# A 46-column unit with its high and low weights in one stationary tile, and a last projection whose last two weight rows go tile by tile

## The chip, the cores and the metric

The kernel runs on one core of one Trainium2 chip, as one program. The metric is the device time of a run in microseconds (us); of several runs the median counts. A separate execution is recorded by the hardware profiler: every instruction of each engine with start and length. The engines are TensorE (PE, with weight loads as PEld), VectorE (DVE), ScalarE (ACT), GpSimd (POOL) and SyncE (SP), which here issues the DMAs.

## What is computed

Two blocks of a language model on a sequence of 512 tokens of width 1024 in float32. The first (a short convolution, a gated delta rule and a convolutional feed-forward) is not touched by the change. The second is:

```python
def second_block(x, w_in, norm_g, pool_w, pool_scale, fox_bf, w_out, final_g):
    ...
        h = rmsnorm_2(x, norm_g[layer])
        z = jnp.einsum('bld,dc->blc', h, w_in[layer])
        (pv, pg, dq, dk, dv, dg, iq, ik, iw, fq, fk, fv, fg, ff) = split_columns(z)
        a_out = pool_mixer(pv, pool_w[layer], pool_scale[layer]) * jax.nn.silu(pg)
        b_o = dsa_mixer(..., iq.reshape(B, L, IDX_HEADS, IDX_DIM), ik, iw * idx_w_scale, topk)
        ...
        log_f = jax.nn.log_sigmoid(ff.astype(jnp.float32) + fox_bf[layer].astype(jnp.float32))
        c_o = fox_mixer(fq..., fk..., fv..., log_f)     # F = cumsum(log_f); logit + F[t] - F[s]
        ...
        mixed = jnp.concatenate([a_out, b_out, c_out], axis=-1)
        x = x + jnp.einsum('blc,cd->bld', mixed, w_out[layer])
    return rmsnorm_2(x, final_g)
```

`dsa_mixer` scores each key for each query, `score = sum_h iw[h] * relu(iq[h] . ik)` over 8 index heads of 32, takes the 128 best keys and attends to those. `ik` has 32 columns of the projection, `iw` 8, and `ff`, the forget gates of `fox_mixer`, 6: these 46 columns are the thin unit.

## The kernel before

**Weights in two parts.** Each float32 weight matrix is used as a rounded high part and the rest, the low part, and so are the activations. A product is then three matmuls of 128x512: high by high, low by high, high by low. SyncE loads a unit of weights (128 columns by 1024 rows, as 128 partitions x 8 x 128) into one of four buffers of `raw`; ScalarE copies it to `whi` (L1190, `split`); VectorE, for some units GpSimd, subtracts to get `wlo` (L1653, L2534). `whi` and `wlo` have two buffers each, so the split of a unit waits for the end of the unit two before it (`unit_done`), and the unit itself waits for its low part (`split_ready`). TensorE multiplies in `unit` (L679), 24 matmuls with the eight blocks of activations, into one of four banks of `gb`.

**The projection into the second block** has the units of `Z_UNITS`, u = 0, 1, 2 and so on: unit 0 is the thin one, units 1 and 2 are `iq`, then come the keys, queries, values and gates of the heads. A unit is written in four quarters, and `schedule()` puts small jobs behind quarters: `put(u, m, job)` stands behind quarter m (from 0) of unit u. Each engine goes through the same plan and does its own share of each job (`beside`), at its own place among its splits and its reads of finished units (`z_out`, in the loop at quarter 1 of the next unit). All waits are semaphores, and every engine does its instructions in the order in which they are written. What reads a finished unit scales it by the norm of each token; this row comes from sums of squares (`third_sums`, four float32 matmuls with `ones`, after quarter 1 of unit 0), VectorE's `sum_positions`, GpSimd's power and the job `spread 2`.

The jobs of the thin unit:
- `turn_iw` (2, 1): ScalarE copies the 32 rows of `ik` four times into `ik4` (`dec`, L1562), TensorE transposes the unit (L1032), and VectorE takes `iw` and `ff` from it (L2199 to L2205). `spread 3` (2, 2) makes the row of the final norm.
- `log_f` (3, 1): the logarithm of the forget gates, a long chain of small VectorE operations (L1658 to L2217).
- `cum_f` (4, 1): TensorE sums them over the positions (L1038, L1039) into bank 3 of `gd`, and VectorE copies the 24 columns out (L2224, semaphore `f_tok`), ahead of its `z_out` in that place.
- `turn_f` (4, 3): TensorE transposes the sums (L1044), ScalarE copies them to `frow` (L1569, `f_rows`), and SyncE sends them to DRAM and back as rows.
- `four`: four score products at once (L1061), one for each of four index heads, one in each bank of `gd`, from slot 14 = (3, 2) on; ScalarE applies relu (L1576), and VectorE adds them up weighted (`score`, L2232, L2235). The third group, n = 8 at (4, 2), uses bank 3 and waits for `f_tok`; the fourth, n = 12 at (5, 0), waits for `f_rows`.

**The last projection** (from L1137) has eight rows of `w_out` as moving operands and the four tiles of 128 tokens as stationary ones; all four tiles of 128x1024 results stand in the eight banks at once. `products(i, c)` is the work of weight row i on tile c, six matmuls (L1158). Weight rows go in the order of i, and within one all four tiles. After a tile's last matmul (`tile_done`) ScalarE squares it and sums (L1637), GpSimd makes the factor (L2546, L2547), VectorE multiplies by factor and `final_g` (L2386), and SyncE sends the 512 KB (L658).

## Time and profile before

| what | us |
|---|---|
| runs of the kernel before | 1306.73, 1307.70, 1307.81 |
| median | 1307.7 |
| span of the profiled execution | 1305.9 |
| TensorE busy in it | 1288.1 (99%) |
| VectorE busy | 822.2 (63%) |
| ScalarE busy | 560.4 (43%) |
| GpSimd busy | 240.9 (18%) |

For the profiled execution the profile gives its span, from the first to the last instruction or transfer, and no separate time; what a run takes around its span is in the runs and not in the span. Matmuls overlap, so the length of one is more than the distance to the next, and a busy TensorE need not be at its peak. The second block's projection begins at 1001.3 us of the span, the last projection near 1255.

### The profile page before, as it was taken

Reading aid. Unit: us, or ns where it says so; the run is one execution under the profiler, and the core shown is the slowest. Engines: PE = TensorE matmul, PEld = TensorE weight load, DVE = VectorE, ACT = ScalarE, POOL = GpSimd, SP = SyncE. Lnnn points to the kernel's source line nnn. Section 1 sums busy time; section 2 is a strip of 40 time slices with the busy share of each in tenths; the row PEclk is TensorE's granted clock in tenths of the full one; section 3 lists DMA queues with packets and bytes.
Section 4 is the critical chain, followed back from the end, with each engine's and each line's share of the span. In section 5 each row is a group of like instructions: output and inputs, shape, how many; then the busy total and the mean of one; then the engine's idle time right before and its main releaser. Section 6 shows DMA issues by size and latency. Waiting matters only on the chain.

```text
span 1305.9 us, 20263 instructions
## 1 busy us (share of the span) xinstructions
PE 1288.1 (99%) x6833; PEld 1029.2 (79%) x6833; DVE 822.2 (63%) x1694; ACT 560.4 (43%) x1010; POOL 240.9 (18%) x491
## 2 busy tenths in 40 slices
PE   8999999999999999999999999999999999999998
PEld 6877878878788788888788888888887766767786
DVE  6976667676676753445477773377755688885823
ACT  5654535445454432223344442244444454434422
POOL 2513304032140400001300000000022234433210
PEclk9999999999999999999999999999999999999999
DMA  6323232232232223333233323433234332222221
GB/s 184 90 66 90 80 86 76 79 87 71 83 88 65 79 81 97 96 96 97 81 104 99 97 74 97 122 93 97 72 91 112 90 107 86 66 65 65 65 65 65
DMA packets 210052, 114.44 MB, mean 88 GB/s; under 512 B 7696, under 2 KB 206671, under 8 KB 210005
## 3 DMA queue, kind: packets, MB, share of 16 engines
q1 hardware_dynamic: 210005, 113.84, 30.2%
q8 instruction: 26, 0.43, 0.1%
q14 instruction: 21, 0.17, 0.0%
HBM read 111.70 MB, written 2.13 MB: 87 GB/s over the span
## 4 chain that ended last, share of the span: by engine, by line
PE 91%; DVE 6%; issue 1%; ACT 1%; DMA 0%; POOL 0%; SPq 0%; POOLq 0%; DVEq 0%; ACTq 0%
PE gb L679 77%; PE gb L1158 2%; PE gd L1158 1%; PE gd L1109 1%; PE gd L1086 1%; PE gd L1099 1%; DVE wlo L1653 1%; DVE selb L2246 1%; PE gd L787 1%; PE gd L870 1%; PE gd L879 1%; DVE small L2245 0%; PE gd L775 0%; DVE selb L2235 0%; PE gd L858 0%
## 5 line engine op out<-in xcount | busy, mean ns | idle before, releaser
L679 PE MATMUL gb<-act_a,whi 128*128 128x512 f32 x2656 | 898.6, 400 | 1.2 <-POOL wlo L2534 0.7
L679 PEld LDWEIGHTS gb<-act_a,whi 128*128 128x128 f32 x2656 | 499.6, 188 | 118.6 <-issue 16.7
L679 PE MATMUL gb<-act_a,wlo 128*128 128x512 f32 x1416 | 552.7, 390 | 0.0
L1653 DVE TENSOR_TENSOR wlo<-raw,whi 128x1024 fp32r<-128x1024 f32 (+1 forms) x198 | 239.2, 1208 | 161.0 <-ACT whi L1190 158.2
L1190 ACT ACTIVATE whi<-raw 128x1024 fp32r<-128x1024 f32 (+1 forms) x211 | 217.2, 1029 | 234.1 <-PE gb L679 203.2
L679 PEld LDWEIGHTS gb<-act_a,wlo 128*128 128x128 f32 x1416 | 266.9, 189 | 48.5 <-issue 1.0
L679 PE MATMUL gb<-act_b,whi 128*128 128x512 f32 x432 | 152.4, 393 | 0.1
L679 PEld LDWEIGHTS gb<-act_b,whi 128*128 128x128 f32 x432 | 81.1, 188 | 17.4 <-DVE qc L1930 0.5
L2488 POOL TENSOR_TENSOR zs<-zs,ca 128x512 f32<-128x512 f32 x3 | 4.2, 1400 | 321.7 <-ACT ca L1193 321.7
L679 PE MATMUL gb<-act_b,wlo 128*128 128x512 f32 x128 | 49.9, 390 | 0.0
L2439 POOL TENSOR_TENSOR elt<-Ti,Ue 128x60 f32<-128x60 f32 (+14 forms) x120 | 44.3, 370 | 27.8 <-DVE Ti L1775 13.5
L2442 POOL TENSOR_TENSOR Ue<-Ue,elt 128x60 f32<-128x60 f32 (+14 forms) x120 | 39.1, 326 | 9.4
L1604 ACT ACTIVATE pT<-gd 128x512 f32<-128x512 f32 (+3 forms) x24 | 10.5, 438 | 61.0 <-PE gd L1099 40.2
L2534 POOL TENSOR_TENSOR wlo<-raw,whi 128x1024 fp32r<-128x1024 f32 x13 | 31.1, 2393 | 22.0 <-ACT whi L1190 22.0
L1289 ACT ACTIVATE ob<-gd,hc 128x128 f32<-128x128 f32 x24 | 8.8, 368 | 55.7 <-DVE Rr L1880 55.7
L2126 DVE TENSOR_TENSOR Yb<-gb,Vt 128x512 f32<-128x512 f32 x22 | 15.2, 691 | 24.9 <-PE gb L679 24.9
L2471 POOL TENSOR_TENSOR zs<-zs,ca 128x512 f32<-128x512 f32 x3 | 5.6, 1858 | 134.8 <-ACT ca L1193 134.8
L2456 POOL TENSOR_TENSOR rr<-ss,rr 128x4 f32<-128x4 f32 x8 | 1.6, 201 | 150.7 <-DVE ss L1899 150.7
L679 PEld LDWEIGHTS gb<-act_b,wlo 128*128 128x128 f32 x128 | 24.0, 188 | 4.6
L2165 DVE TENSOR_TENSOR xT<-xT,gb 128x512 f32 (+1 forms) x16 | 11.0, 688 | 26.3 <-PE gb L679 26.3
L2245 DVE MAX8 small<-selb 128x8 f32<-128x256 f32 (+2 forms) x48 | 26.6, 555 | 0.6
L2450 POOL TENSOR_TENSOR rr<-ss,eps_one 128x4 f32<-128x4 f32 x8 | 1.6, 202 | 134.1 <-DVE ss L1823 134.1
(508 smaller groups left out, 1573.2 us busy)
## 6 DMA issues: line engine op xcount, KB each, us to landing
raw<-in_w_in_dram SPq DMA_DIRECT2D x102, 512.0 KB, 3.4
raw<-in_w_up_dram SPq DMA_DIRECT2D x44, 512.0 KB, 3.6
raw<-in_w_down_dram SPq DMA_DIRECT2D x16, 384.0 KB, 3.1
raw<-in_w_down_dram SPq DMA_DIRECT2D x16, 320.0 KB, 3.0
raw<-in_w_a_out_dram SPq DMA_DIRECT2D x8, 512.0 KB, 3.4
raw<-in_w_b_out_dram SPq DMA_DIRECT2D x8, 512.0 KB, 3.4
raw<-in_w_o_dram SPq DMA_DIRECT2D x8, 512.0 KB, 3.4
raw<-in_w_out_dram SPq DMA_DIRECT2D x8, 512.0 KB, 3.5
```

The costliest lines, as they stand in the source:

```text
L679: ins = pe.matmul(gb[:, b, :], l, r, start=(first and m == 0), stop=(last and m == len(todo) - 1))
L787: ins = pe.matmul(gd[:, 3, c * P:c * P + P], KT[:, c, :], QT[:, c, :], start=True, stop=True)
L870: pe.matmul(gd[:, 3, 0:P], Ui[:, c, :], rhs, start=True, stop=True).then_inc(vn_done, 1)
L879: pe.matmul(gd[:, 1, 0:P], AT[:, c, :], vn[:], start=True, stop=True).then_inc(av_done, 1)
L1158: ins = pe.matmul(place(c, half), l, r, start=False, stop=(i == KD - 1 and m == 2), skip_group_check=True)
L1190: sc.activation(whi[:, i % 2, 0:k * P], raw[:, i % 4, 0:k * P], ACT.Copy).then_inc(hi_ready, 1)
L1653: dve.tensor_tensor(wlo[:, i % 2, 0:k * P], raw[:, i % 4, 0:k * P], whi[:, i % 2, 0:k * P].bitcast(F32), ALU.subtract).then_inc(split_read ...
L2126: dve.tensor_tensor(scaled[s], gb[:, 2 * q + s, :], flat(Vt), ALU.mult).then_inc(up_scaled, 1)
L2245: link(dve.max(small[:, 0:8], v))
L2439: pool.tensor_tensor(elt[:, :, 0:n], row_at(m), Ue[:, :, m:m + 1].to_broadcast([P, TC, n]), ALU.mult).then_inc(el_used, 1)
L2442: pool.tensor_tensor(Ue[:, :, m + 1:E], Ue[:, :, m + 1:E], elt[:, :, 0:n], ALU.subtract).then_inc(el_done, 1)
L2534: pool.tensor_tensor(wlo[:, n % 2, :], raw[:, n % 4, :], whi[:, n % 2, :].bitcast(F32), ALU.subtract).then_inc(split_ready, 1)
```

## The change

Part one, the thin unit. The 46 columns are loaded in two DMAs of 16 and 40 columns (before: 64 and 64). ScalarE writes their high parts to columns 0 to 45 of each block of `whi` and VectorE the low parts to columns 64 to 109 of the same block. The unit is then two matmuls per block of activations, 16 and not 24, whose result has the high weights' share in rows 0 to 45 and the low weights' in rows 64 to 109. Where the results are read the two are added: ScalarE copies the low rows of `ik` aside, VectorE adds them into `ik4`, and ScalarE makes the three other copies; `iw` and `ff` are added up by two more small VectorE operations. `third_sums` stands after quarter 2 of the 16 (again twelve matmuls), and six jobs of the plan stand two quarters later.

Part two, the last projection. Weight rows 6 and 7 are done for tiles 0 and 1 one after the other, and then tile 2 with both rows and tile 3 with both. The last tile is squared, multiplied and sent in halves of 512 columns: VectorE multiplies both halves by `final_g`, then VectorE scales the first and ScalarE the second.

```diff
+THIN = B_FQ - B_IK + HX
+THIN_LOW = P // 2
...
-    put(2, 1, ("turn_iw",))
+    put(2, 3, ("turn_iw",))
...
+        ik_low = flat(LT)[0:32, :]
...
-                    sp.dma_start(dst[:, :, 64:P], w2[:, :, B_END - 64:B_END]).then_inc(iw_extra, 16)
-                    sp.wait_ge(iw_extra, 16)
-                    sp.dma_start(dst[:, :, 0:64], w2[:, :, B_IK:B_IK + 64]).then_inc(raw_landed[n % 4], 16)
+                    sp.dma_start(dst[:, :, THIN - 16:THIN], w2[:, :, B_END - 16:B_END]).then_inc(late_landed, 16)
+                    sp.wait_ge(late_landed, 16)
+                    sp.dma_start(dst[:, :, 0:B_FQ - B_IK], w2[:, :, B_IK:B_FQ]).then_inc(raw_landed[n % 4], 16)
...
-            for c in range(TC):
+            for c in range(TC - 1):
                 sp.wait_ge(outs_ready, c + 1)
                 sp.dma_start(out[0, c * P:c * P + P, :], outs[:, c, :]).then_inc(out_sent, 16)
-            sp.wait_ge(out_sent, 16 * TC)
+            for half, (done, count) in enumerate(((out_half, 1), (outs_ready, TC + 1))):
+                sp.wait_ge(done, count)
+                cols = slice(half * T, half * T + T)
+                sp.dma_start(out[0, (TC - 1) * P:TC * P, cols], outs[:, TC - 1, cols]).then_inc(out_sent, 16)
...
-                    todo += [(hi, a), (lo, a), (hi, c)]
+                    todo += [(hi, a), (hi, c)] if packed else [(hi, a), (lo, a), (hi, c)]
...
-                        pe.wait_ge(ik_ready, 1)
+                        pe.wait_ge(ik_ready, 3)
...
-                    if (u, m) == (0, 1):
+                    if (u, m) == (0, 2):
                         third_sums()
...
+                    if i == KD - 1 and (half == 1 or c == TC - 1):
+                        ins.then_inc(tile_done, 1)
...
-            for i in range(1, KD):
+            for i in range(1, KD - 2):
...
+            pe.wait_ge(split_ready, N_W + KD - 1)
+            pe.wait_ge(m_lo, KD - 1)
+            products(KD - 2, 0)
+            products(KD - 2, 1)
+            pe.wait_ge(split_ready, N_W + KD)
+            pe.wait_ge(m_lo, KD)
+            products(KD - 1, 0)
+            products(KD - 1, 1)
+            for c in range(2, TC):
+                products(KD - 2, c)
+                products(KD - 1, c)
...
                 elif what == "turn_iw":
                     sc.wait_ge(z_read, 1)
-                    for i in range(4):
-                        ins = sc.activation(ik4[32 * i:32 * i + 32, :], flat(iwff)[0:32, :], ACT.Copy)
+                    sc.activation(ik_low, flat(iwff)[THIN_LOW:THIN_LOW + 32, :], ACT.Copy).then_inc(ik_ready, 1)
+                    sc.wait_ge(ik_ready, 2)
+                    for i in range(1, 4):
+                        ins = sc.activation(ik4[32 * i:32 * i + 32, :], ik4[0:32, :], ACT.Copy)
                     ins.then_inc(ik_ready, 1)
...
+            for half in range(2):
+                sc.wait_ge(tile_done, TC + half)
+                sc.activation(wk[:, half * T:half * T + T], gd[:, 2 + half, :], ACT.Square,
+                              accum_out=small[:, 19 + half:20 + half]).then_inc(osq, 1)
+            sc.wait_ge(orr, TC)
+            sc.wait_ge(outs_ready, TC)
+            sc.activation(outs[:, TC - 1, T:2 * T], outs[:, TC - 1, T:2 * T], ACT.Copy,
+                          scale=small[:, 36 + TC - 1:36 + TC]).then_inc(outs_ready, 1)
...
                 if what == "turn_iw":
+                    dve.wait_ge(ik_ready, 1)
+                    dve.tensor_tensor(ik4[0:32, :], flat(iwff)[0:32, :], ik_low, ALU.add).then_inc(ik_ready, 1)
                     dve.wait_ge(iw_turned, 1)
...
+            for half in range(2):
+                dve.wait_ge(osq, TC + half)
+                ins = dve.tensor_tensor(outs[:, TC - 1, half * T:half * T + T], gd[:, 2 + half, :],
+                                        gfin[:, half * T:half * T + T], ALU.mult)
...
+            ins.then_inc(outs_ready, 1)
+            dve.wait_ge(orr, TC)
+            dve.tensor_scalar(outs[:, TC - 1, 0:T], outs[:, TC - 1, 0:T], small[:, 36 + TC - 1:36 + TC], None,
+                              ALU.mult).then_inc(out_half, 1)
...
+                if c == TC - 1:
+                    pool.wait_ge(osq, TC + 1)
+                    link(pool.tensor_scalar(small[:, 40 + c:41 + c], small[:, 20:21], 1.0 / D, small[:, 40 + c:41 + c],
+                                            ALU.mult, ALU.add))
```

The other lines of the plan that move: `spread 2` from (1, 2) to (2, 0), `spread 3` from (2, 2) to (3, 0), `log_f` from (3, 1) to (3, 2), `cum_f` from (4, 1) to (4, 2), `turn_f` from (4, 3) to (5, 0). The groups of score products keep their places.

What this makes of the order on the engines, at three places. The line numbers of the kernel after are higher: L1050 and L1051 are `cum_f`, L1073 the score products, L1056 `turn_f`, L2272 the copy of the sums. The first place is TensorE in unit 4, before:

```order
L1038 MATMUL gd<-sm,triu 128x24 [waits relu_ready,f_ready]
L1039 MATMUL gd<-sm,ones 128x24
L679 MATMUL gb<-act_a,whi 128x512
L679 MATMUL gb<-act_a,wlo 128x512
L679 MATMUL gb<-act_a,whi 128x512 x2
L679 MATMUL gb<-act_a,wlo 128x512
L679 MATMUL gb<-act_a,whi 128x512
L1061 MATMUL gd<-dec,KT 128x384 [waits f_tok,relu_ready]
L1061 MATMUL gd<-dec,KT 128x384 x3
```

TensorE in unit 4, after:

```order
L691 MATMUL gb<-act_a,whi 128x512 x2
L691 MATMUL gb<-act_a,wlo 128x512
L691 MATMUL gb<-act_a,whi 128x512
L1050 MATMUL gd<-sm,triu 128x24 [waits relu_ready,f_ready]
L1051 MATMUL gd<-sm,ones 128x24
L1073 MATMUL gd<-dec,KT 128x384 [waits f_tok,relu_ready]
L1073 MATMUL gd<-dec,KT 128x384 x3
```

The six products that stood between the sums and the third group of score products now stand ahead of the sums.

The second place is VectorE in the same unit, before (`selb` holds the scores of VectorE, `gate` is unit 3 being read):

```order
L2235 SCALAR_TENSOR_TENSOR selb<-zs,sm,selb 128x256 [waits relu_used,relu_ready]
L2224 COPY sm<-gd 128x24 [waits f_cum]
L2306 SCALAR_TENSOR_TENSOR gate<-gb,wk 128x512 [waits pads_ready,unit_done]
L2235 SCALAR_TENSOR_TENSOR selb<-qc,sm,selb 128x256 [waits relu_used,relu_ready]
L2235 SCALAR_TENSOR_TENSOR selb<-kc,sm,selb 128x256 [waits relu_used,relu_ready]
L2240 MEMSET selb 64x64 [waits relu_used]
L2232 TENSOR_SCALAR selb<-Yb,sm 128x384 [waits relu_ready,dve_order]
```

VectorE in the same unit, after:

```order
L2283 SCALAR_TENSOR_TENSOR selb<-zs,sm,selb 128x256 [waits relu_used,relu_ready]
L2354 SCALAR_TENSOR_TENSOR gate<-gb,wk 128x512 [waits pads_ready,unit_done]
L2283 SCALAR_TENSOR_TENSOR selb<-qc,sm,selb 128x256 [waits relu_used,relu_ready]
L2283 SCALAR_TENSOR_TENSOR selb<-kc,sm,selb 128x256 [waits relu_used,relu_ready]
L2288 MEMSET selb 64x64 [waits relu_used]
L2272 COPY sm<-gd 128x24 [waits f_cum,dve_order]
L2280 TENSOR_SCALAR selb<-Yb,sm 128x384 [waits relu_ready]
```

The copy of the sums moved behind the reading of unit 3, two scores and the memset.

The third place is TensorE from unit 4 to unit 5, before:

```order
L1044 MATMUL gd<-ident,sm 6x128 [waits relu_ready,f_tok]
L1044 MATMUL gd<-ident,sm 6x128 x3
L679 MATMUL gb<-act_a,whi 128x512 [waits split_ready,z_read]
L679 MATMUL gb<-act_a,wlo 128x512
L679 MATMUL gb<-act_a,whi 128x512 x2
L679 MATMUL gb<-act_a,wlo 128x512
L679 MATMUL gb<-act_a,whi 128x512
L1061 MATMUL gd<-dec,QT 128x384 [waits f_rows,relu_ready]
```

TensorE from unit 4 to unit 5, after:

```order
L691 MATMUL gb<-act_a,whi 128x512 [waits split_ready,z_read]
L691 MATMUL gb<-act_a,wlo 128x512
L691 MATMUL gb<-act_a,whi 128x512 x2
L691 MATMUL gb<-act_a,wlo 128x512
L691 MATMUL gb<-act_a,whi 128x512
L1056 MATMUL gd<-ident,sm 6x128 [waits relu_ready,f_tok]
L1056 MATMUL gd<-ident,sm 6x128 x3
L1073 MATMUL gd<-dec,QT 128x384 [waits f_rows,relu_ready]
```

The transposes now stand directly ahead of the fourth group, and on ScalarE the copy to `frow` stands behind the split of the next unit where it stood ahead of it.

## Rows read from the trace of the kernel before

**Rows 1.** Page, part 4: shares of the chain that ended last, by engine

```profile
PE 91%; DVE 6%; issue 1%; ACT 1%; DMA 0%; POOL 0%; SPq 0%; POOLq 0%; DVEq 0%; ACTq 0%
```

**Rows 2.** Timeline, PE, unit 0: start us, us, engine, line, tiles, count, [idle before]

```profile
1004.02 1.02 PE L691 MATMUL gd<-zs,ones 128*128 128x512 f32 x2
...
1007.05 0.79 PE L679 MATMUL gb<-act_a,whi 128*128 128x512 f32 x1
1007.68 0.39 PE L679 MATMUL gb<-act_a,wlo 128*128 128x512 f32 x1
...
1010.44 0.39 PE L679 MATMUL gb<-act_a,wlo 128*128 128x512 f32 x1
```

**Rows 3.** Timeline, DVE: first sum over positions, and unit 1's low weights

```profile
1006.79 0.69 DVE L1677 TENSOR_TENSOR Yb<-gd,ident 128x512 f32<-128x512 f32 x1 [3.07 <-PE gd L691]
...
1008.45 1.23 DVE L1653 TENSOR_TENSOR wlo<-raw,whi 128x1024 fp32r<-128x1024 f32 x1
```

**Rows 4.** Timeline, PE: sums, third group, transposes, fourth group

```profile
1033.60 0.37 PE L1038 MATMUL gd<-sm,triu 128*128 128x24 f32 x2
...
1035.60 0.93 PE L1061 MATMUL gd<-dec,KT 32*128 32x384 f32 x8
...
1038.00 0.60 PE L1044 MATMUL gd<-ident,sm 128*6 128x128 f32 x4
...
1039.92 0.93 PE L1061 MATMUL gd<-dec,QT 32*128 32x384 f32 x8
```

**Rows 5.** Timeline, DVE: start of the logarithm, copy of the sums, end of scores

```profile
1026.50 0.17 DVE L1658 TENSOR_SCALAR sm<-sm 128x24 f32<-128x24 f32 x1
...
1035.08 0.17 DVE L2224 COPY sm<-gd 128x24 f32<-128x24 f32 x1
...
1036.90 0.11 DVE L2240 MEMSET selb<- 64x64 f32 x1
```

**Rows 6.** Timeline, ACT: key copies, final row, split of unit 4, exponential, turned row

```profile
1017.79 2.54 ACT L1562 ACTIVATE dec<-Ui 32x512 f32<-32x512 f32 x4
1022.21 0.60 ACT L1558 ACTIVATE wk<-gd 128x512 f32<-128x512 f32 x1 [1.88 <-PE gd L697]
1023.66 1.06 ACT L1190 ACTIVATE whi<-raw 128x1024 fp32r<-128x1024 f32 x1 [0.85 <-PE gb L679]
...
1026.03 0.22 ACT L1566 ACTIVATE sm<-sm 128x24 f32<-128x24 f32 x1
...
1038.64 0.59 ACT L1569 ACTIVATE frow<-gd 6x512 f32<-6x512 f32 x1 [0.40 <-PE gd L1044]
```

**Rows 7.** Timeline of PE; stretches: engines busy, PEclk, DMA share, GB/s

```profile
1171.67 0.67 PE L1099 MATMUL gd<-ident,qc 128*128 128x128 f32 x3 [2.69 <-DVE qc L2273]
...
1168.00:1171.60 3.60, 0.98 (x5) 0.46 (x3) 3.50 (x8) 0.00 (x0) 0.15 (x1) 1.00 0.34 93
1172.00:1175.00 3.00, 3.00 (x11) 2.31 (x9) 1.86 (x5) 1.94 (x5) 0.00 (x0) 0.50 0.06 17
```

**Rows 8.** Timeline, all engines: last weight split, and the end

```profile
1289.80 1.23 DVE L1653 TENSOR_TENSOR wlo<-raw,whi 128x1024 fp32r<-128x1024 f32 x1 [4.21 <-ACT whi L1190]
...
1299.10 0.39 PE L1158 MATMUL gd<-wlo,act_a 128*128 128x512 f32 x1
...
1299.52 1.02 ACT L1637 ACTIVATE wk<-gd 128x1024 f32<-128x1024 f32 x1 [0.24 <-PE gd L1158]
...
1300.23 2.64 DVE L2386 SCALAR_TENSOR_TENSOR gate<-gd,small,gfin 128x1024 f32<-128x1024 f32 x2
...
1301.00 0.55 POOL L2547 TENSOR_TENSOR small<-small,mhalf 128x1 f32<-128x1 f32 x1
```

**Rows 9.** DMA issues (count, KB each, us to landing); last, one stretch

```profile
out_dram<-gate SPq DMA_DIRECT2D x4, 512.0 KB, 2.6
...
pw<-in_pool_w_dram SPq DMA_DIRECT2D x4, 16.0 KB, 2.1
...
1304.00:1305.00 1.00, 0.00 (x0) 0.00 (x0) 0.00 (x0) 0.00 (x0) 0.00 (x0) 0.50 0.99 406
```

More of the change, by code:

```diff
@@ L104, in schedule @@
     put = lambda u, m, e: at.setdefault((u, m), []).append(e)
-    put(1, 2, ("spread", 2))
-    put(2, 1, ("turn_iw",))
-    put(2, 2, ("spread", 3))
-    put(3, 1, ("log_f",))
-    put(4, 1, ("cum_f",))
-    put(4, 3, ("turn_f",))
+    put(2, 0, ("spread", 2))
+    put(2, 3, ("turn_iw",))
+    put(3, 0, ("spread", 3))
+    put(3, 2, ("log_f",))
+    put(4, 2, ("cum_f",))
+    put(5, 0, ("turn_f",))
     todo = [(c, h) for c in range(1, TC) for h in range(IDX_HEADS)]
@@ L1123, in _ @@
                 p = unit(N_Z + u, N_Z + u, u % 4, 0, H_HI, H_LO, parts=4,
-                         ready=(h_ready, 2 * KD) if u == 0 else None, high=(hn_hi, 2 * KD) if u == 0 else None)
+                         ready=(h_ready, 2 * KD) if u == 0 else None, high=(hn_hi, 2 * KD) if u == 0 else None,
+                         packed=(u == 0))
                 for m in range(4):
                     next(p)
-                    if (u, m) == (0, 1):
+                    if (u, m) == (0, 2):
                         third_sums()
@@ L1189, in split @@
                     sc.wait_ge(unit_done, n - 1)
-                sc.activation(whi[:, i % 2, 0:k * P], raw[:, i % 4, 0:k * P], ACT.Copy).then_inc(hi_ready, 1)
+                if isinstance(n, int) and n == N_Z:
+                    sc.activation(thin_part(whi[:, i % 2, :], 0), thin_part(raw[:, i % 4, :], 0), ACT.Copy).then_inc(hi_ready, 1)
+                else:
+                    sc.activation(whi[:, i % 2, 0:k * P], raw[:, i % 4, 0:k * P], ACT.Copy).then_inc(hi_ready, 1)
             def norm_square(dst, src, gain=1.0):
@@ L1652, in split @@
                     dve.wait_ge(split_ready, n)
-                dve.tensor_tensor(wlo[:, i % 2, 0:k * P], raw[:, i % 4, 0:k * P],
-                                  whi[:, i % 2, 0:k * P].bitcast(F32), ALU.subtract).then_inc(split_ready, 1)
+                if isinstance(n, int) and n == N_Z:
+                    dve.tensor_tensor(thin_part(whi[:, i % 2, :], THIN_LOW), thin_part(raw[:, i % 4, :], 0),
+                                      thin_part(whi[:, i % 2, :], 0).bitcast(F32), ALU.subtract).then_inc(split_ready, 1)
+                else:
+                    dve.tensor_tensor(wlo[:, i % 2, 0:k * P], raw[:, i % 4, 0:k * P],
+                                      whi[:, i % 2, 0:k * P].bitcast(F32), ALU.subtract).then_inc(split_ready, 1)
             def log1p(e, s, t, out_):
@@ L2198, in beside @@
                     col = lambda i, k: sm[:, i, 0:TC * k].rearrange("p (c h) -> p c h", h=k)
-                    dve.tensor_scalar(col(8, IDX_HEADS), t[:, :, B_IW - B_IK:B_IW - B_IK + IDX_HEADS], float(IDX_HEADS) ** -0.5, None, ALU.mult)
-                    link(dve.tensor_tensor(col(4, HX), t[:, :, P - HX:P],
+                    iw_at, ff_at, scale = B_IW - B_IK, THIN - HX, float(IDX_HEADS) ** -0.5
+                    dve.tensor_scalar(col(8, IDX_HEADS), t[:, :, iw_at:iw_at + IDX_HEADS], scale, None, ALU.mult)
+                    link(dve.tensor_tensor(col(4, HX), t[:, :, ff_at:ff_at + HX],
                                            rows8[:, 16:16 + HX].unsqueeze(1).to_broadcast([P, TC, HX]), ALU.add))
+                    iw_at, ff_at = iw_at + THIN_LOW, ff_at + THIN_LOW
+                    dve.scalar_tensor_tensor(col(8, IDX_HEADS), t[:, :, iw_at:iw_at + IDX_HEADS], scale, col(8, IDX_HEADS),
+                                             ALU.mult, ALU.add)
+                    link(dve.tensor_tensor(col(4, HX), t[:, :, ff_at:ff_at + HX], col(4, HX), ALU.add))
                     n = HX * TC
@@ L2381, in _ @@
                 split(N_W + i, N_W + i)
-            dve.wait_ge(late_landed, 16 * 5)
-            for c in range(TC):
+            dve.wait_ge(late_landed, 16 * 6)
+            for c in range(TC - 1):
                 dve.wait_ge(orr, c + 1)
```

33 lines of the change are left out of this document (19 added, 14 removed).

## The prediction, made before the changed kernel ran

> **What bounds the kernel now.** I read the chain of work that ended last first: TensorE holds 91% of it [rows 1]. So a matmul taken away is worth its whole pitch, but only where nothing else that TensorE waits for ends later, and a new wait on TensorE costs its whole length. Then I read TensorE, VectorE and ScalarE in order of time around the thin unit, because the change moves small jobs there by half a unit, and last the way from the final product to the end. There is one execution with a profile; its span is 1305.9 us, the median of the three runs 1307.7 us, so 1.8 us lie around the span and I keep them as they are. All sums below are made on the span.
>
> **Thin unit: eight products fewer.** The products run at a pitch of (1010.44 - 1007.68) / 12 = 0.23 us [rows 2]. Eight fewer are worth 1.8 us if TensorE can go on. It can't go on at once. The four sums of squares still follow the twelfth product of the unit, so they start at 1004.02 as before, and behind them now stand four products of the thin unit instead of twelve: TensorE would want unit 1 at 1007.05 + 0.63 + 3 x 0.23 = 1008.4. Unit 1 needs its low weights, and VectorE makes them only after the reduction of the first sum, from 1008.45 to 1009.68 [rows 3]. Nothing in the change moves that. TensorE stands from 1008.4 to about 1009.75, so of 1.8 us about 0.45 are left. The thinner splits (46 columns of 128) and the smaller loads lie ahead of that, under the products of the previous unit, and give nothing; the 64-byte and 160-byte packets have, like the two halves before, several us of cover.
>
> **The small jobs moved by half a unit.** I followed each to see what it is late for.
> - The token row comes 2.3 us later (0.45 earlier unit start against twelve more products ahead of it), and with it z_out of the thin unit and the split behind it on VectorE; that split ends near 1020.3. TensorE wants unit 3 at about 1022.0: before, ScalarE's split at unit 2's end started at 1023.66 [rows 6], and TensorE is now 0.45 earlier and has the spread of 0.9 still ahead of it. Covered by 1.7.
> - The key rows: ScalarE copies the low part, VectorE adds it behind that split and z_out (a sum of 512 columns takes 0.69 [rows 3]), until about 1021.5; then ScalarE makes three copies. Four took 2.54, so three take 1.9, until about 1023.4. The split for unit 4, the final row (0.60) and the exponential follow on ScalarE in that order, which puts the exponential at about 1026.2 where it was at 1026.03 [rows 6]. The logarithm on VectorE therefore starts near 1026.5 as before [rows 5]. The two extra small additions (0.2 each) lie ahead of that in idle time.
> - **The cumulative sum** is where the change costs. Before, VectorE copied it out (0.17) ahead of z_out and two scores, at 1035.08, while TensorE did six products between the sum (1033.60) and the third group of four score products (1035.60) [rows 4, 5]. Now the sum stands directly ahead of that group, which waits for the copy, and on VectorE the copy stands behind z_out, two scores and the memset of 1036.90. VectorE is busy without a gap from 1026.50 to there, so the copy can't come forward; it starts a tenth after the memset begins, less the 0.1 that the copy itself took earlier, say at 1037.0, and the score products start at about 1037.25. Free, TensorE would be there at 1035.60 - 0.45 = 1035.15, since what it does up to there is otherwise the same in another order. So it stands 2.1 us there, and is 1.65 behind the kernel before. Behind the waiting product are all of the next units' products, since TensorE takes matmuls in order; VectorE and ScalarE wait in turn for these scores.
> - **The turned row.** Before, six products lay between the transposes (1038.00) and the fourth group (1039.92), which waits for ScalarE's copy of the row: 0.64 until the copy starts and 0.59 for it [rows 4, 6]. Now nothing lies between. Transposes to copied row is 1.25, and with the way back 1.3, against 0.35 for the transposes alone: a second wait of 0.9. The split now standing ahead of the copy on ScalarE starts about 1.1 before the transposes do and so is just done. Sum so far: 1.65 + 0.9 = 2.55, less an estimated 0.15 because transposes and score products now stand side by side, with one change fewer between long products and small ones. I take **+2.4**.
> - Does it stay? VectorE had idle time just after (it waited for score copies), so it can't catch up by itself; it is delayed with TensorE. Where TensorE later waits for VectorE (2.69 at 1171.67 [rows 7]), VectorE is as late. So I carry the 2.4 to the end. The bounds are 1.5 (the copy done early, half of the second wait covered) and 3.0.
>
> **The end.** The last product starts at 1299.10; then come ScalarE 1.03 and the read of its sum, GpSimd until 1301.55, VectorE's second product of the pair until 1302.87 and the transfer, 2.6 from issue [rows 8, 9]. After the change the last tile's first half is squared under the last three products. The second half takes 0.60 instead of 1.03 (as the final row's copy of 512 columns [rows 6]): 0.4 saved. GpSimd needs one operation more, 0.2 with its link of 0.1. VectorE multiplies tile 2 until 1300.15 as its tile is done 1.4 us earlier; the two halves without scale follow (0.69 each [rows 3]) and end at 1301.5, so after the scale (1301.15) and not before it. Then ScalarE scales one half (0.60 to 0.70) and VectorE the other side by side. The second half is issued at about 1302.3 instead of 1302.9: 0.6. It is 256 KB instead of 512. Four transfers follow each other at 406 GB/s [rows 9], where 512 KB are 1.3 us; half is 0.65 less, but the first half, issued 0.35 earlier, is in its way: 0.3 net. The bounds for the transfer are 2.6 (no gain) and the 2.1 that 16 KB take [rows 9]. I take 2.3, so the end gives **-0.9**, bounds -0.5 and -1.3.
>
> The rule that speaks against this part is in the Trainium skill, DMA: Bandwidth & Descriptors, section Anatomy of one DMA (written for GpSimd's path, while SyncE issues here): about 2.0 us of each are fixed, and two halves pay it twice, though side by side. By it the 2.6 would be 0.6 of movement and halving gain 0.3 at most; the end would give the same 0.9 by it, with no room for the -1.3. No row here shows a 256 KB write.
>
> The tile-by-tile order needs the weights of the last row after 12 products, not 24: at 1299.10 - 35 x 0.227 = 1291.2. VectorE has them at 1289.80 + 1.23 = 1291.03 [rows 8]. That is 0.1 to spare; I take +0.05.
>
> **Sum:** 2.4 - 0.9 + 0.05 = +1.55 on the span (the 0.45 of the thin unit is in the 2.4), so 1307.5 for the span and **1309.3** for the time.
>
> **Rivals.**
> - *A: as summed, TensorE's clock stays at 2.4 GHz.* 1309.3, spread 1308.3 to 1310.3.
> - *B: the long new wait also lowers the clock.* At 1171.67 TensorE had been idle for 2.69 us; from 1172 to 1175 its granted clock was 0.50, which is 1.2 GHz, and then full again [rows 7]. Three us at half speed are 1.5 us of work lost. The new wait of 2.1 us plus the tiny sums ahead of it is nearly as long as that one. If the clock falls here, TensorE is late for the fourth group as well and nothing absorbs it: 1309.3 + 1.5 = 1310.8. It decides the sign of the verdict: from a total of +2.6 on, that is slower. The Trainium skill, TensorE: Matmul & The Clock Gate, section HAM oscillation, describes this fall after pauses between bursts; by that rule, the trace agrees.
> - *C: the waits are not there,* because VectorE reaches the copy early enough or the delay is taken up by later waits on others. Then the thin unit gives 0.45 and the end 0.85: 1306.4. Against it stands the order on VectorE and its gapless row of work.
> - *D: the waits are not there and unit 1's weights are early too:* 1307.7 - 1.8 - 0.85 = 1305.0. Nothing in the trace speaks for it, since the first wait stands on operations that the change leaves alone.
>
> **Chances.** A 0.58, B 0.30, C 0.09, D 0.03. A measurement of this kernel tells about 0.2%, 2.6 us, from no change. Slower by more than that (above 1310.3) holds most of B and the upper edge of A: 0.32. Faster by more (below 1305.1) is D and little else: 0.04. Within 0.2%: 0.64. The range runs from below A's low edge, for the case that the clock's earlier fall at 1172 is spared, to the middle upper part of B: 1307.0 to 1311.3; C and D are left out.
>
> **What would show it.** In the profile after: TensorE idle near 1.4 us ahead of unit 1, released by VectorE's split; idle near 2 us ahead of the third group of score products, released by the copy of 24 columns; idle near 0.9 ahead of the fourth, released by ScalarE's row; the granted clock just after the second of these (below 1.00 is B); span from the last product to the end 5.9 instead of 6.8. It would be wrong if VectorE's copy stood earlier in time than 1036.5, if the wait at 1171.67 were shorter by what came in earlier, or if that earlier wait lost its own fall of the clock, which alone moves the time by 1.5 us either way.

## The result, and the profile after

| | before | after |
|---|---|---|
| median of 11 runs each, us | 1307.67 | 1309.85 |
| lowest to highest, us | 1306.23 to 1308.02 | 1308.05 to 1312.22 |
| span of the profiled execution, us | 1305.9 | 1308.0 |
| ratio | | 1.0025 (95% interval 1.0017 to 1.0033) |

The changed kernel took 1309.85 us where 1309.3 was forecast, inside the range of 1307.0 to 1311.3. It is 2.2 us slower than the kernel before, or 0.25%. The whole interval of the ratio lies above 1, so the loss is small but real.

First the four longest waits of TensorE in the second block, in the profile after (engine, tile and line that waited, whom for, us in total, times, longest):

```profile
PE gd L1111 <- DVE qc L2321: 3.5, 2, 2.7
PE gd L1073 <- DVE sm L2272: 2.7, 1, 2.7
PE gb L691 <- DVE wlo L1695: 1.2, 1, 1.2
PE gd L1073 <- ACT frow L1597: 0.8, 1, 0.8
```

The first was there before [rows 7]. The other three are new: unit 1 waits for its low weights, the third group of score products for the copied sums, the fourth for the turned row. In order of time on TensorE:

```profile
1009.83 0.50 PE L691 MATMUL gb<-act_a,whi 128*128 128x512 f32 x1 [1.18 <-DVE wlo L1695]
...
1034.42 0.30 PE L1050 MATMUL gd<-sm,triu 128*128 128x24 f32 x2
1034.56 0.38 PE L1051 MATMUL gd<-sm,ones 128*128 128x24 f32 x2
1037.62 0.93 PE L1073 MATMUL gd<-dec,KT 32*128 32x384 f32 x8 [2.68 <-DVE sm L2272]
1038.48 0.79 PE L691 MATMUL gb<-act_a,whi 128*128 128x512 f32 x1
1039.07 0.63 PE L691 MATMUL gb<-act_a,wlo 128*128 128x512 f32 x1
...
1042.92 0.60 PE L1056 MATMUL gd<-ident,sm 128*6 128x128 f32 x4
1044.29 0.93 PE L1073 MATMUL gd<-dec,QT 32*128 32x384 f32 x8 [0.77 <-ACT frow L1597]
```

The third group is 2.0 us later than before (1035.60 in [rows 4]), the fourth 4.4 (1039.92); 0.1 of each is there from the start, since this profile is 0.11 later already at the sums of squares of unit 0. Between the two groups the products of 1038.48, 1039.07 and 1039.50 stand 0.59 and 0.43 apart, where 0.23 is the pitch. The granted clock is 0.57 in this stretch, so it was 1.2 GHz for most of it. Behind the old wait, which now ends at 1175.92, the clock is 1.00, where [rows 7] had 0.50 (stretch, its length, busy us of PE, PEld, DVE, ACT and POOL, clock, DMA share, GB/s):

```profile
1038.00:1041.50 3.50, 3.50 (x15) 2.44 (x8) 2.07 (x4) 1.64 (x4) 0.00 (x0) 0.57 0.00 0
1172.00:1175.00 3.00, 1.22 (x6) 0.65 (x4) 2.93 (x5) 0.00 (x0) 0.41 (x1) 1.00 0.11 15
1175.00:1178.00 3.00, 2.08 (x13) 1.77 (x13) 2.96 (x9) 1.00 (x2) 0.00 (x0) 1.00 0.56 159
```

VectorE just ahead of the third group. The copy of the sums (L2272) is the last row, behind the memset; in [rows 5] it was at 1035.08:

```profile
1035.41 0.69 DVE L2354 SCALAR_TENSOR_TENSOR gate<-gb,wk 128x512 f32<-128x512 f32 x1
1036.01 0.48 DVE L2283 SCALAR_TENSOR_TENSOR selb<-qc,sm,selb 128x256 f32<-128x256 f32 x1
1036.59 0.48 DVE L2283 SCALAR_TENSOR_TENSOR selb<-kc,sm,selb 128x256 f32<-128x256 f32 x1
1037.15 0.11 DVE L2288 MEMSET selb<- 64x64 f32 x1
1037.29 0.18 DVE L2272 COPY sm<-gd 128x24 f32<-128x24 f32 x1
```

The end, from the last product on, all engines:

```profile
1302.16 0.39 PE L1171 MATMUL gd<-wlo,act_a 128*128 128x512 f32 x1
...
1302.58 0.60 ACT L1671 ACTIVATE wk<-gd 128x512 f32<-128x512 f32 x1
...
1303.13 1.41 DVE L2438 TENSOR_TENSOR gate<-gd,gfin 128x512 f32<-128x512 f32 x2
...
1303.80 0.55 POOL L2609 TENSOR_TENSOR small<-small,mhalf 128x1 f32<-128x1 f32 x1
1304.45 0.48 DVE L2444 TENSOR_SCALAR gate<-gate,small 128x512 f32<-128x512 f32 x1
1304.63 0.72 ACT L1675 ACTIVATE gate<-gate,small 128x512 f32<-128x512 f32 x1 [1.35 <-DVE gate L2438]
```

From the last product to the end of the span it is 5.84 us, where it was 1305.9 - 1299.10 = 6.80 (spans are given to a tenth, so such a length is good to about 0.05). VectorE's two products end about when GpSimd has the factor, and only the scaling by the factor is left then, in halves on two engines. The transfers (count, KB, us to landing):

```profile
out_dram<-gate SPq DMA_DIRECT2D x3, 512.0 KB, 2.6
...
out_dram<-gate SPq DMA_DIRECT2D x2, 256.0 KB, 2.1
```

### The profile page after: what moved, and what is told of

Same layout as the page of the kernel before. It is cut to its first block, busy times and chain, and to the rows that moved or that the text cites. A ratio compares the mean times of both kernels' runs of the same rounds, so it can differ in the third digit from the quotient of the medians.

```text
span 1308.0 us, 20260 instructions
## 1 busy us (share of the span) xinstructions
PE 1287.0 (98%) x6825; PEld 1029.4 (79%) x6825; DVE 823.3 (63%) x1699; ACT 561.1 (43%) x1013; POOL 240.5 (18%) x492
## 4 chain that ended last, share of the span: by engine, by line
PE 89%; DVE 6%; issue 2%; ACT 2%; DMA 0%; POOL 0%; DVEq 0%; ACTq 0%; POOLq 0%
PE gb L691 75%; PE gb L1171 2%; PE gd L1171 1%; PE gd L1121 1%; PE gd L1098 1%; DVE wlo L1695 1%; PE gd L1111 1%; DVE selb L2294 1%; PE gd L799 1%; PE gd L882 1%; PE gd L891 1%; DVE selb L2283 1%; DVE small L2293 0%; PE gd L787 0%; ACT whi L1216 0%
```

## The experiments

Each was timed over up to 11 runs beside the kernel before on the same chip. Profiles start the second block a few tenths apart. So where two are compared below, the way is taken from the start of the sums of squares in unit 0 (1004.02 in [rows 2], 1004.13 in the changed kernel), called the mark here, to the start of the last product. The kernel before has 1299.10 - 1004.02 = 295.08 for it, the changed kernel 1302.16 - 1004.13 = 298.03. A fall is a stretch in which the granted clock is 0.50.

**1. The sums and the turned row back in their old places.** From the changed kernel:

```diff
-    put(4, 2, ("cum_f",))
+    put(4, 1, ("cum_f",))
-    put(5, 0, ("turn_f",))
+    put(4, 3, ("turn_f",))
```

> The changed kernel with two lines of the plan set back: the cumulative sum at (4, 1) and the turned row at (4, 3); the packed unit and the end stay. My theory is that both new waits come from these two lines. The sum will then wait for ScalarE's eighth score copy (1033.8) and stand near 1033.9, the third group near 1035.9 instead of 1037.62, with no wait on the copy of 24 columns, no fall of the clock near 1038 and no wait for the row; the fourth group near 1040.2 instead of 1044.29. Time: 1307.7 + 0.3 - 0.9 = 1307.1 us. Rival: the work that the packed unit adds (copies, additions, later exponential) is the cost; then the time stays at 1309 to 1310.

Measured: 1306.75 (1305.71 to 1307.01), ratio 0.9994 (0.9985 to 1.0003). The waits ahead of the third and fourth groups are gone, and the fall at 1038 with them, so these are what the change costs. But from mark to last product it is 295.08, to the hundredth what the kernel before has (both with a fall near 1172): the thin unit brings nothing at all. TensorE loses its gain in two waits, the 1.18 ahead of unit 1 as in the changed kernel, and a new one ahead of the sums:

```profile
1033.87 0.37 PE L1050 MATMUL gd<-sm,triu 128*128 128x24 f32 x2 [0.74 <-ACT kc L1604]
```

ScalarE's relu copies wait in turn for VectorE's scores, and those stand behind the logarithm. It starts at 1026.75, which is 22.71 after the mark, where [rows 5] has 22.48.

**2. Only VectorE's copy early.** TensorE's order is that of the changed kernel; VectorE takes the copy ahead of its reading of unit 3 again:

```diff
-                    early = [e for e in plan.get((u, m), ()) if e[0] == "cum_f"]
+                    early = [("cum_f",)] if (u, m) == (4, 1) else []
```

> The changed kernel with one thing moved on VectorE alone: the copy of the 24 sums stands at (4, 1) again, ahead of the reading of unit 3; TensorE's order is untouched. If VectorE's place of the copy is what the first wait is made of, the wait ahead of the third group shrinks from 2.68 to about 0.9 (copy near 1035.6) and the clock keeps 1.00 there; the wait for the row (0.8) stays. Time: 1307.7 + 0.3 + 0.8 - 0.9 = 1307.9 us. If TensorE's order is what costs, the wait stays above 2 and the time at 1309 to 1310.

Measured: 1307.55 (1306.22 to 1307.67), ratio 0.9997 (0.9988 to 1.0006). TensorE in that profile:

```profile
1035.80 0.93 PE L1073 MATMUL gd<-dec,KT 32*128 32x384 f32 x8 [0.79 <-DVE sm L2272]
...
1040.90 0.93 PE L1073 MATMUL gd<-dec,QT 32*128 32x384 f32 x8 [0.77 <-ACT frow L1597]
```

One copy of 24 columns, done 1.8 us earlier on VectorE, takes the first wait from 2.68 to 0.79, and the clock stays at 1.00 behind it. This settles which instruction TensorE stood for. (The clock did fall behind the old wait, near 1174.)

**3. Only the turned row back at (4, 3).**

```diff
-    put(5, 0, ("turn_f",))
+    put(4, 3, ("turn_f",))
```

> The changed kernel with one job put back: the turned row (TensorE's four transposes and ScalarE's copy to frow) stands behind quarter 3 of unit 4 as in the kernel before; the sums stay at (4, 2). It asks what the second wait costs by itself. By my theory the wait of 0.8 us ahead of the fourth group goes (six products stand there again) and the one of 2.7 ahead of the third stays: 0.8 us less than the changed kernel, about 1309.0, with TensorE idle about 2.7 us ahead of the third group and not ahead of the fourth. Rival: the copy to frow, now ahead of the split of the next unit on ScalarE, delays that split and the next unit waits instead, so nothing is gained: 1309.8. On the clock: if a wait of 2.7 us lowers it by itself, it falls here after the third group, to 0.50 for 3 us; if it needs the second wait near it, it stays at 1.00 and the time is 1.5 lower still, 1307.5.

Measured: 1310.09 (1309.03 to 1311.28), ratio 1.0019 (1.0010 to 1.0028). The wait is gone; the groups are 43.50 - 37.64 = 5.86 apart where the changed kernel has 6.67:

```profile
1037.64 0.93 PE L1073 MATMUL gd<-dec,KT 32*128 32x384 f32 x8 [2.67 <-DVE sm L2272]
1041.13 1.05 PE L1056 MATMUL gd<-ident,sm 128*6 128x128 f32 x4
1043.50 0.93 PE L1073 MATMUL gd<-dec,QT 32*128 32x384 f32 x8
```

The 0.8 is there in the profile and not in the median, which is 1.1 over the forecast. In this profile the clock fell behind both long waits, at 1038 us and at 1175 us; the changed kernel's fell once. So the wait of 2.67 doesn't need the second one near it to be followed by a fall:

```profile
1038.00:1041.50 3.50, 3.50 (x16) 2.10 (x9) 2.05 (x4) 1.64 (x4) 0.00 (x0) 0.59 0.02 5
...
1175.00:1178.00 3.00, 2.87 (x9) 2.39 (x10) 2.31 (x7) 1.79 (x5) 0.00 (x0) 0.53 0.31 92
```

**4. Part one alone**, with the last projection and the end of the kernel before (no diff: it is part one of the change).

> Part one alone: thin unit and plan of the changed kernel, with the last projection and the end of the kernel before. It measures the term of +2.4 us directly, which the prediction carries to the end. With what the traces have shown since (waits of 2.7 and 0.8, and a fall of the clock that moved from 1172 us to the third group) I expect 3.1 us over the kernel before, 1310.7, and 0.9 us over the changed kernel. Rival: the end of the changed kernel gains nothing once part one is there, because VectorE or GpSimd are late by then; then it is as the changed kernel, 1309.8.

Measured, in 6 runs: 1310.54 (1308.82 to 1312.97), ratio 1.0029 (1.0017 to 1.0041). As forecast within 0.2. Its profile is worth more, because in it the clock never fell between the mark and the last product, although the waits of 2.67 and 0.77 are there, and the old one of 2.71:

```profile
1037.35 0.93 PE L1069 MATMUL gd<-dec,KT 32*128 32x384 f32 x8 [2.67 <-DVE sm L2248]
...
1041.04 0.60 PE L1052 MATMUL gd<-ident,sm 128*6 128x128 f32 x4
1042.41 0.93 PE L1069 MATMUL gd<-dec,QT 32*128 32x384 f32 x8 [0.77 <-ACT frow L1583]
...
1300.30 0.39 PE L1167 MATMUL gd<-wlo,act_a 128*128 128x512 f32 x1
```

```profile
1038.00:1041.50 3.50, 3.50 (x20) 2.52 (x16) 2.34 (x5) 2.67 (x5) 0.00 (x0) 1.00 0.02 5
```

**5. Part two alone**, on the kernel before.

> The kernel before with only the second part of the change: last two weight rows tile by tile, last tile in halves. From the last product's start to the end 5.85 us instead of 6.8, and the time 1307.7 - 0.9 = 1306.8 us. Rival: the halves pay the transfer's fixed time twice and the gain seen in the profile of the whole change was chance; then 1307.7.

Measured: 1306.67 (1305.56 to 1306.99), ratio 0.9992 (0.9983 to 1.0001). That is 0.9 less than the 1307.60 of the kernel before beside it, as forecast. From last product to end it is 1304.0 - 1298.14 = 5.86. Here too the profile has no fall, behind the very wait that had one in [rows 7]:

```profile
1171.87 0.55 PE L1103 MATMUL gd<-ident,qc 128*128 128x128 f32 x3 [2.68 <-DVE qc L2297]
...
1298.14 0.39 PE L1162 MATMUL gd<-wlo,act_a 128*128 128x512 f32 x1
```

**6. Only the six lines of the plan**, on the kernel before (thin unit of 24 products, old end):

```diff
-    put(4, 1, ("cum_f",))
-    put(4, 3, ("turn_f",))
+    put(4, 2, ("cum_f",))
+    put(5, 0, ("turn_f",))
```

and the other four moves. Three of the six jobs stand two quarters later by this (`spread 2`, `turn_iw`, `spread 3`), and `log_f`, `cum_f` and `turn_f` one quarter. It is the same in the changed kernel, where I wrote two quarters for all six.

> The kernel before with only the plan's six lines as after the change: 24 products in the thin unit, no packing, old end. If the plan carries the cost, the third group waits 2 us or more for the copy (it starts near 1037.2), the fourth waits 0.8 for the row, and the time is 1307.7 + 1.6 + 0.8 = 1310.1 us, 1311.6 where the clock falls once more. If the packing's own extra work carries it, the waits are under 0.5 and the time within 0.5 of 1307.7.

Measured, in 9 runs: 1311.12 (1309.51 to 1313.65), ratio 1.0027 (1.0017 to 1.0037), between the 1310.1 without and the 1311.6 with one more fall. The plan alone makes both waits, 2.69 and 0.8. In this profile the clock was down for over 6 us, by its mean of 0.57 over the eight us of the last line:

```profile
1038.08 1.66 PE L1061 MATMUL gd<-dec,KT 32*128 32x384 f32 x8 [2.69 <-DVE sm L2224]
```

```profile
1038.00:1041.50 3.50, 3.42 (x12) 2.03 (x13) 1.04 (x2) 1.64 (x4) 0.00 (x0) 0.50 0.00 0
...
1037.00:1045.00 8.00, 6.92 (x23) 4.64 (x24) 4.27 (x8) 2.70 (x5) 0.00 (x0) 0.57 0.00 0
```

**7. Halves without the tile-by-tile order.** From the changed kernel:

```diff
-            for i in range(1, KD - 2):
+            for i in range(1, KD):
...
-            products(KD - 2, 0)
-            products(KD - 2, 1)
...
-            for c in range(2, TC):
-                products(KD - 2, c)
-                products(KD - 1, c)
```

> The changed kernel with weight rows 6 and 7 again row by row over all four tiles; the last tile is still squared, scaled and sent in halves. It parts the gain of the end (0.9 us) into order and halves. In the old order the tiles end 1.36 us apart (six products each), which is less than VectorE's product of 1.41 for a tile, and tile 3's first half is done only three products ahead of the last one, as in the new order. Theory of the prediction: halves need the new order, since VectorE multiplies tile 2 until 1.4 us later than there: last product to end 6.5 us where the changed kernel has 5.84 and the kernel before 6.8, and the time 0.6 over the changed kernel, 1310.4. Rival: VectorE isn't what the end waits for, and the halves alone bring all: 1309.8.

Measured, in 5 runs: 1312.00 (1311.03 to 1313.6), ratio 1.0037 (1.0023 to 1.0050). The time is 1.6 over the 1310.4 I expected. 0.7 of it is the end; the profiled run, with one short fall, took 1311.05, and the slower ones have a lower mean clock. From last product to end it is 1309.3 - 1302.10 = 7.20, worse than the 6.80 of before and than the 6.5 I expected:

```profile
1303.22 1.28 DVE L2424 SCALAR_TENSOR_TENSOR gate<-gd,small,gfin 128x1024 f32<-128x1024 f32 x1
...
1304.11 0.55 POOL L2599 TENSOR_TENSOR small<-small,mhalf 128x1 f32<-128x1 f32 x1
1304.43 1.41 DVE L2428 TENSOR_TENSOR gate<-gd,gfin 128x512 f32<-128x512 f32 x2
1305.75 0.48 DVE L2434 TENSOR_SCALAR gate<-gate,small 128x512 f32<-128x512 f32 x1
1305.93 0.72 ACT L1665 ACTIVATE gate<-gate,small 128x512 f32<-128x512 f32 x1 [2.35 <-DVE gate L2428]
```

VectorE still has tile 2 until 1304.4. The factor is ready at 1304.66, so the two products without it (1.41) are nearly all in addition: ScalarE ends 1306.65 - 1302.10 = 4.55 after the last product, where VectorE ended 3.77 after it in the kernel before.

**8. Order without halves:** the last tile is squared, multiplied and sent whole.

> The changed kernel with the last tile whole again (one square, one product by VectorE, one transfer of 512 KB), but weight rows 6 and 7 still tile by tile. Theory: the order alone brings only that VectorE is free in time for the last tile, which it was before within 0.25 us; last product to end 6.5 to 6.8 us against 5.84, time 0.7 to 0.9 over the changed kernel, 1310.5 to 1310.7. Rival: the free VectorE brings most of it, 6.2 or less and 1310.1 or less. With the run of the halves alone this tells whether the two parts of the end add up or need each other.

Measured, in 5 runs: 1313.12 (1311.62 to 1313.41), ratio 1.0036 (1.0022 to 1.0050). Last product to end: 1311.5 - 1304.73 = 6.77, as forecast; the time is 2.5 over the forecast. The clock was down for over 6 us at 1037 to 1044 and again near 1177 in this profile, where the changed kernel had one short fall; from mark to last product it has 300.61 against 298.03, so the excess lies there and not in the end. The end shows VectorE idle instead of late:

```profile
1307.21 1.28 DVE L2420 SCALAR_TENSOR_TENSOR gate<-gd,small,gfin 128x1024 f32<-128x1024 f32 x1 [1.43 <-POOL small L2581]
```

So order alone gives nothing (0.03, less than the rounding), halves alone lose 0.40, both together give 0.96. They aren't two savings but one: the order makes the idle VectorE, and the halves fill it.

**9. Low weights of unit 1 first.** From experiment 1's kernel, one line moved:

```diff
+            split(N_Z + 1, N_Z + 1)
             sum_positions(0, Yb)
             link(mean_square())
-            split(N_Z + 1, N_Z + 1)
```

> The kernel with the sums and the turned row back in their old places (thin unit and end as changed), and one line moved: VectorE makes the low weights of unit 1 ahead of the first sum over positions, not behind it. VectorE is idle there from 1003.75 to 1006.82 while ScalarE has the high weights at 1005.04, so the 1.22 us fit in whole and the sum isn't later. It asks whether the wait of 1.18 ahead of unit 1 is all that holds back the eight saved products. Theory: the wait goes, and with it ScalarE's and VectorE's chain to the exponential (table load, log, scores) comes forward too, because each link of it follows TensorE: exponential at 1025.3 where it was at 1026.49, and 1.2 us less than the version without this line: 1305.6. Rival: something on the chain does not follow TensorE (GpSimd's power of the token row, ready at 1014.2, or the three key copies), the exponential stays within 0.3 of 1026.5 and TensorE loses the 1.2 again ahead of the sums: 1306.8.

Measured: 1305.36 (1304.02 to 1305.68), ratio 0.9986 (0.9977 to 0.9995). It beats both kernels, the kernel before by 1.35 us beside it on the same chip (25 runs, median 1306.71). From mark to last product: 1298.07 - 1004.32 = 293.75, 1.33 less than without the line (both profiles have one fall, near 1172), and the exponential is at 1025.33. TensorE no longer waits ahead of unit 1. My reason was half wrong: the line stands behind the wait for the sums of squares, so VectorE makes the weights not in its idle time but right after it, and the sum over positions is 1.1 later:

```profile
1007.10 1.23 DVE L1695 TENSOR_TENSOR wlo<-raw,whi 128x1024 fp32r<-128x1024 f32 x1 [3.07 <-PE gd L703]
```

That delay reaches nobody: GpSimd starts the power of the token row 7.25 us after the mark with the line and without it. The wait of 0.7 ahead of the cumulative sums is still there and moved along.

**10. The same line in the changed kernel.**

> The changed kernel with only that line moved (low weights of unit 1 ahead of the first sum over positions); sums and turned row stay in the changed places. Theory: TensorE is 1.2 us earlier at unit 1, and the wait of 2.7 ahead of the third group stays 2.7, since TensorE's and VectorE's way to it both come forward: 1308.6, waits 2.7 and 0.8. Rival: VectorE's row of work from the logarithm on doesn't come forward, then the wait is 3.9 and the time as the changed kernel, 1309.8.

Measured: 1308.35 (1306.50 to 1310.84), ratio 1.0012 (1.0003 to 1.0021). The waits ahead of the third and fourth groups are 2.70 and 0.77. TensorE's and VectorE's ways to the third group both came forward (from the mark to the group it is 32.07, against 33.49 in the changed kernel), and the gain was not swallowed there: from mark to last product it is 1300.72 - 1004.07 = 296.65, 1.38 less than the changed kernel, each with one fall at the third group.

```profile
1036.14 1.36 PE L1073 MATMUL gd<-dec,KT 32*128 32x384 f32 x8 [2.70 <-DVE sm L2272]
```

**11. The changed kernel once more**, unedited, for the clock.

> The changed kernel once more, nothing edited: a second profiled execution and more times, for the granted clock. Theory: the waits (1.2, 2.7, 0.8 and 2.7 near 1176) come back to the hundredth, since they are set by the order of the work, while the falls of the clock behind them need not come back at the same places; the times fall again on few values near 1308, 1309.7 and 1311.8, by none, one or more falls. Rival: the fall belongs to the place, then it is again from 1038.5 to 1041.8 and not near 1176, and the spread of times has another source.

Measured, in 9 runs: 1310.58 (1308.14 to 1312.17), ratio 1.0027 (1.0017 to 1.0037). The waits came back within 0.02. The clock fell at the third group again and not near 1176, which is what the rival said; but it began over half a us earlier, before the group and not after it (1.66 for the eight matmuls, not 0.93). So neither the theory nor the rival holds in whole.

```profile
1037.62 1.66 PE L1073 MATMUL gd<-dec,KT 32*128 32x384 f32 x8 [2.68 <-DVE sm L2272]
```

**What the clock costs.** Each run has a mean granted clock of its own, and the times of a kernel lie on rough steps by it:

| kernel | clock 1.000 | next step | next |
|---|---|---|---|
| changed (first 11 runs) | 1308.05 | 1309.59 to 1309.85 (0.997, 0.998; 5 runs) | 1311.5 to 1312.22 (0.996; 5 runs) |
| experiment 10 | 1306.50 to 1306.90 (3) | 1308.29 to 1308.35 (0.998, 0.999; 4) | 1309.14 to 1310.84 (0.995 to 0.997; 4) |

The mean tells the falls only roughly. In all 13 profiles the clock also falls after the last product, where TensorE has nothing left to do and the fall costs nothing; in the kernel before this tail is longer than the fall that counts. That its runs of 1306.4 to 1306.8 us have means from 0.998 to 1.000 fits this. The tail in the profile of the kernel before (the first length after the comma is TensorE's busy time):

```profile
1302.50:1304.00 1.50, 0.00 (x0) 0.00 (x0) 0.37 (x1) 0.00 (x0) 0.00 (x0) 0.50 0.96 393
```

What one fall costs is read from the profiles. At the third group it is 1.6: from mark to last product the changed kernel has 298.03 and experiment 4, with the same waits and no fall, 296.47. A fall near 1172 costs 1.1, by 295.08 against 1298.14 - 1004.11 = 294.03 in experiment 5. TensorE loses 1.6 there at first too: after the wait it starts four matmuls of `gate` at 1176.85 in the kernel before and at 1175.45 in experiment 5, and this wait had ended 0.20 later in experiment 5. But 0.3 of that comes back two us later, where TensorE without a fall waits for VectorE and TensorE with a fall does not (experiment 5, then the kernel before):

```profile
1179.09 0.66 PE L1103 MATMUL gd<-ident,Yb 128*128 128x128 f32 x4 [0.17 <-DVE Yb L2297]
...
1180.15 0.60 PE L1099 MATMUL gd<-ident,Yb 128*128 128x128 f32 x4
```

The rest, 0.2, comes back later on; I have not traced where.

Eight profiles have the wait of 2.7 at the third group, and seven of them a fall with it (all but experiment 4). Thirteen have the wait of 2.7 near 1172 to 1178; seven have a fall there (before, experiments 1, 2, 3, 6, 8, 9) and six don't (after, 4, 5, 7, 10, 11). The lengths, 2.67 to 2.71, don't tell the two apart: 2.68 was followed by a fall in experiment 3 and by none in experiment 5.

## Why the prediction came out right

The time (1309.3 against 1309.85), the sign and the mechanism held; the closeness of the time is partly luck, as the points on part one and on the clock say. Times below are the profile's own; the profile after is 0.11 later at the mark. By the steps of the prediction:

- **Thin unit, 0.45 left of 1.8.** The wait ahead of unit 1 was as said: TensorE is idle for 1.18, and unit 1 starts at 1009.83 for the 1009.75 of the sum. Experiment 9 takes this wait away and gains 1.33 of the 1.8. The 0.45 that I counted as left are not: experiment 1 keeps nothing of them, since the logarithm started 0.2 later after the mark while TensorE came earlier, and TensorE gave them up in the wait ahead of the sums.
- **Small jobs covered.** The exponential came at 1026.58, forecast 1026.2, and the logarithm at 1026.83, forecast 1026.5. The key copies ended at 1023.56 where I had 1023.4, and the split, the final row's copy and the table load behind them took 3.02 until the exponential where I had 2.8. Less the 0.11 of the mark, the logarithm was 0.2 late, and VectorE's gapless row carried this 0.2 to the copy of the sums.
- **The wait for the copy.** Forecast 2.1, measured 2.68. This is the term that was mis-sized: the copy began at 1037.29, not 1037.0, and the third group at 1037.62, not 1037.25; TensorE was there at 1034.94, not 1035.15. Counted from the mark, the group is 33.49 - 31.58 = 1.91 later than before, where I had 1.65. The mechanism, one tiny copy that moved behind the reading of unit 3, two scores and a memset, is shown by experiment 2, and that the plan alone makes it by experiment 6.
- **The turned row.** Forecast 0.9, measured 0.77, and gone in experiment 3.
- **Part one +2.4, nothing absorbs it.** With no fall of the clock on either side, experiments 4 and 5 give 296.47 - 294.03 = 2.44 from the mark to the last product. At the fourth group it is 2.7 (38.58 from the mark against 35.90), where the working had 2.55, and 0.2 of it was absorbed on the way, near 1070, though I had said that nothing is; the 0.15 that I took off had another reason, which no run shows. The wait for the copy was 0.6 longer than forecast, but 0.3 of that is TensorE's earlier arrival and costs nothing, and the wait for the row was 0.1 shorter. The term is right partly by luck.
- **The end -0.9.** Measured -0.96. Before, VectorE ended 1302.87 - 1299.10 = 3.77 after the last product; now ScalarE ends 1305.35 - 1302.16 = 3.19 after it, the 0.6 of the sum. The rest, 0.38, is the transfer, forecast 0.3: the first half landed in 2.0 and the second, issued 0.4 behind it, in 2.2, where 512 KB take 2.6. That order and halves need each other was in the working for VectorE (tile 2 until 1300.15) and is now shown by experiments 7 and 8. The working left GpSimd's extra 0.2 out of the 1301.15 for the scale; the factor was ready 2.19 after the last product and VectorE's two products ended 2.38 after it, so nothing hung on it. The weights of the last row came late for a weight load by 0.17 and for no product.
- **The fixed part of a transfer.** From the Trainium skill, DMA: Bandwidth & Descriptors, section Anatomy of one DMA, I took only the fixed 2.0 us and set it against the 2.6 of the trace. The page's own fit adds the bytes at 436 GB/s to it, which gives, as estimates, 3.2 us for 512 KB and 2.6 for 256 KB, and a gain of 0.6 by halving, not 0.3 at most. The measured 2.6 and 2.0 to 2.2 lie below both; the page's fit is for GpSimd's path, and these transfers are SyncE's. From the medians of 2.6 and 2.1 the fixed part would be about 1.6, an estimate.
- **Clock, A against B.** B's event happened, and A's time came out. The clock did fall at the new wait (chance given 0.30), but the old fall near 1172, which the span of before contains, did not come in that profile. So one fall stands against another, and the sum needs none; had the old one stayed, that run would have been near the 1310.8 of B. The sum without any fall, 1.55, compares with runs at a mean clock of 1.000: on the chip of experiments 9 to 11, 1308.14 and 1308.17 of the changed kernel (experiment 11) against 1306.53 of the kernel before, so 1.6. The medians are 2.2 apart. A fall at the new place costs 1.6 where at the old one it costs 1.1, and the changed kernel has runs of up to 1312.2, whose lower mean clock (0.996) points to longer or more falls; those runs have no profile. My price of 1.5 for a fall was right for the new place and too high for the old. The Trainium skill, TensorE: Matmul & The Clock Gate, section HAM oscillation, ties the fall to a long enough pause. The rows here agree in that every fall ahead of the last product came with a pause of 2.7 us; but of 21 such pauses 14 had a fall and seven had none, so the length of the pause alone does not decide it. What tells these apart stays open: no experiment varied only what stood ahead of a pause.

## What to carry to other kernels

When products are taken out of a bound engine, list what that engine will wait for next, and move its producer forward in the same change. Here the eight saved products brought nothing by themselves, and 1.33 of their 1.8 us once one line let VectorE make the next unit's weights first (experiment 9). A tiny operation that moves by a few places in the order of a busy helper engine can cost the bound engine two microseconds, because the price is not its own 0.17 but the row of work that it now stands behind. A last tile in halves paid here only because VectorE, which does the extra pass, would otherwise have stood idle waiting for the factor.

## What the runs showed of the hardware that I had not expected

- Waits of the same length, 2.67 to 2.71 us, were followed by 1.2 GHz in some executions and by 2.4 GHz in others, also where the kernels are the same up to that wait (the changed kernel and experiment 4, the kernel before and experiment 5). A fall of about 3.4 us costs 1.1 to 1.6 us; that was its length in most profiles, and over 6 us in experiments 6 and 8.
- A fall can begin while TensorE is still waiting (the third group took 1.66 in experiments 6, 7, 8 and 11) or about a us after it went on (0.93 in the changed kernel and experiment 3, with the next products slow).
- The 256 KB writes landed in 2.1 us (median of the two), as fast as the 16 KB loads of [rows 9], against 2.6 for 512 KB.
